# A mixture-of-experts tail: picks sorted by expert, two rows a token fetched during the last experts, the other four fetched 32 tokens at a time and summed in four PSUM strips

## The reference

```
scores = sigmoid(h2d @ w_router)                    # (1056, 64), float32
eidx   = top 6 of (scores + bias) inside the best 4 of 8 groups
w      = scores[eidx] / sum(scores[eidx]) * 2.5
routed[t] = sum_k w[t, k] * swiglu(h2d[t], w_gate[e], w_up[e], w_down[e]),  e = eidx[t, k]
out = layer_norm(2 ** 0.25 * h + routed + swiglu(h2d, shared weights))
```

## Time and profile before

| what | value |
|---|---|
| median of 3 plain runs | 1801.19 us (1797.17 to 1805.35) |
| the profiled execution | 1811.97 us |
| its span, first to last instruction | 1809.8 us |
| PE busy | 1740.8 us, 96% of the span |
| DVE busy | 1069.2 us, 59% |
| ACT busy | 678.6 us, 37% |
| POOL busy | 331.7 us, 18% |
| moved by the DMA engines | 409.01 MB, mean 226 GB/s |
| mean granted clock of PE | 0.988 of full |

### The profile page before, as it was taken

The page is one execution under the profiler, slowest core; times in us unless marked ns, Lnnn a source line. Parts: engine busy times, 40 slices in busy tenths (PEclk is TensorE's granted clock), DMA queues, the critical chain, the costliest instruction groups (busy, mean ns, idle before and its releaser), DMA issues. The chain is left out here.

```text
span 1809.8 us, 27145 instructions
## 1 busy us (share of the span) xinstructions
PE 1740.8 (96%) x9472; PEld 1336.0 (74%) x9472; DVE 1069.2 (59%) x1724; ACT 678.6 (37%) x1092; POOL 331.7 (18%) x282
## 2 busy tenths in 40 slices
PE   9999999999999999999996889999999999999996
PEld 9999999999955555998873556767676767676633
DVE  3112442634345565745684657777777777777568
ACT  3112222312244555212110145656565656565411
POOL 0000321412010000000145332222222222222112
PEclk9999999999999999999997999999999999999998
DMA  6332633434223123624260589999999999999697
GB/s 223 93 93 76 169 118 108 145 118 136 74 67 102 40 67 136 244 83 156 92 239 1 181 293 374 394 379 404 396 407 382 398 393 384 397 396 366 226 376 315
DMA packets 140736, 409.01 MB, mean 226 GB/s; under 512 B 29444, under 2 KB 91300, under 8 KB 121060
## 3 DMA queue, kind: packets, MB, share of 16 engines
q1 hardware_dynamic: 116436, 338.38, 50.8%
q0 software_dynamic: 21344, 52.59, 7.6%
q10 hardware_dynamic: 2880, 17.04, 2.3%
HBM read 359.78 MB, written 67.80 MB: 236 GB/s over the span
## 5 line engine op out<-in xcount | busy, mean ns | idle before, releaser
L2675 PE MATMUL e_Y<-mixT,e_aT 128*128 128x512 f32 x544 | 246.7, 596 | 6.8 <-issue 5.8
L2686 PE MATMUL e_G<-w_lo,xT_hi 128*128 128x512 f32 x528 | 205.7, 390 | 0.0
L2675 PEld LDWEIGHTS e_Y<-mixT,e_aT 128*128 128x128 f32 x544 | 103.5, 191 | 112.1 <-issue 107.0
L2533 DVE TENSOR_TENSOR w_lo<-wb,e_w_hi 128x1024 fp32r<-128x1024 f32 x132 | 155.5, 1220 | 16.4 <-ACT e_w_hi L2453 9.5
L2526 DVE TENSOR_TENSOR xT_lo<-e_T,xT_hi 128x1024 fp32r<-128x1024 f32 x66 | 80.8, 1225 | 133.3 <-ACT xT_hi L2448 133.3
L2533 DVE TENSOR_TENSOR w_lo<-wb,half_hi 128x1024 fp32r<-128x1024 f32 x128 | 150.7, 1220 | 10.4 <-ACT half_hi L2453 10.2
L1323 PE MATMUL banks<-x_hi,gw_hi 128*128 128x352 f32 x464 | 151.6, 327 | 1.4 <-DVE r_srg L1115 1.4
L1323 PE MATMUL banks<-x_hi,gw_lo 128*128 128x352 f32 x464 | 148.8, 321 | 0.0
L1323 PE MATMUL banks<-x_lo,gw_hi 128*128 128x352 f32 x464 | 148.8, 321 | 0.0
L2448 ACT CAST xT_hi<-e_T 128x1024 fp32r<-128x1024 f32 x66 | 67.1, 1017 | 206.8 <-PE e_T L2664 206.8
L187 PE MATMUL banks<-w_hi,x_hi 128*128 128x244 f32 x512 | 142.0, 277 | 1.6 <-DVE x_lo L244 1.6
(11 more groups left out here) (436 smaller groups left out, 3604.2 us busy)
## 6 DMA issues: line engine op xcount, KB each, us to landing
wb<-in_w_exp_gu SPq DMA_DIRECT2D x64, 2048.0 KB
mixT<-in_w_exp_dn SPq DMA_DIRECT2D x68, 1024.0 KB
yk<-d_y_rows SPq DMA_DIRECT2D x16, 1536.0 KB, 18.9
gw_sb<-in_w_gate SPq DMA_DIRECT2D x20, 512.0 KB, 7.0
d_proj<-o_sb SPq DMA_DIRECT2D x8, 1098.0 KB, 5.6
d_gateT<-r_g_out ACTq DMA_DIRECT2D x16, 528.0 KB, 2.6
pages<-in_cache_both SPq DMA_DIRECT2D x64, 128.0 KB, 2.0
wb<-in_w_exp_gu ACTq DMA_DIRECT2D x4, 2048.0 KB
```

The lines of the kernel that those rows point to most:

```text
L2533: v.tensor_tensor(w_lo[s][:, :, at_k, :], w_gu[s][:, :, at_k, :], w_hi[c][:, :, at_k, :].bitcast(F32), ALU.subtract).then_inc(w_lo_ok, 1)
L2675: mm = t_.matmul(Y[q][:], aT[:, c, k, :], w_d[:, s, k, q * 512:(q + 1) * 512], start=k == 0, stop=k == 1)
L2686: mm = t_.matmul(G[c], x[:, c, k, :], w[:, :, k, :], start=k == 0 and i == 0, stop=k == KD - 1 and i == 2)
```

## The change

1. `choose` sorts the six picks of a token by expert number, largest first (a copy to float and a MAX8 for each tile). So picks 4 and 5 never belong to the last four experts.
2. The overflow blocks run before the last four experts (60 to 63) and no longer after them. The lists are rearranged on DVE for that.
3. Picks 4 and 5 of each tile (`pair`, one transfer of 1 MB) are loaded during the last group, once the rows of the first 64 blocks have landed, and DVE adds them (`add_row`) at several places: one add after the second block's gated(), three before the last gated(), four around the last two evacuations, eight behind them.
4. Picks 0 to 3 of each tile (`stack`, four transfers of 512 KB) are loaded when all rows have landed. A transfer takes 32 tokens x 4 picks onto 128 partitions, so that partition 4 * token + pick holds one row. PE multiplies such a block with a 128x32 matrix w_stack, in which column i holds the four weights of token i, into 32 PSUM partitions (a strip); four blocks make the tile. Seven stack buffers lie over those of the pairs and the weights; some wait until pairs are added.
5. w_stack is made by DVE (w_masked, before the last group), four small products on PE with a constant matrix `sel` (loaded once, 0.28 MB), and DVE (`stacked_weights`, before the last evacuations). The diagonal matrices (`diag`, L2637) are gone.
6. LAST_ORDER is now 0 to 8, the small tile last; its six transfers come behind all stacks. h tiles 0 and 1 are loaded in trunk in the place of the norm's constants, and the constants during the last group, in the place of those.

```diff
-LAST_ORDER = (NT - 1, *range(NT - 1))
+LAST_ORDER = range(NT)
...
-            sp.dma_start(g1, a["ln2_g"].partition_broadcast(P)).then_inc(ln2_in, 16)
-            sp.dma_start(b1, a["ln2_b"].partition_broadcast(P)).then_inc(ln2_in, 16)
+            for t in range(2):
+                sp.dma_start(early[:, t * D:(t + 1) * D], h_rows[tok(t), :]).then_inc(acc_in[t], 16)
...
-                link(v.tensor_copy(f6[:].rearrange("p (t k) -> p t k", k=TOPK), i8[:, :, 0:TOPK]))
+                link(v.tensor_copy(f8[:, :, 0:TOPK], i8[:, :, 0:TOPK]))
+
+                for t in range(G):
+                    ins = v.max(by_number[:, t, :], f8[:, t, :])
+                link(ins)
+                link(v.tensor_copy(f6[:].rearrange("p (t k) -> p t k", k=TOPK), by_number[:, :, 0:TOPK]))
...
+            def pair(t):
+
+                sp.dma_start(pairs[t][:].rearrange("p k n -> p (k n)"),
+                             y_rows.rearrange("(t k) n -> t (k n)", k=8)[t * P:(t + 1) * P, 4 * D:6 * D]).then_inc(pair_in[t], 16)
+
+            def stack(t):
+
+                b = stack_of[t][0]
+                for q in range(4):
+                    sp.dma_start(stacks[b][:, q, :], y_rows.rearrange("(t k) n -> t k n", k=8)[t * P + NS * q:t * P + NS * (q + 1), 0:4, :]).then_inc(stack_in[b], 16)
...
+            weights_read(0)
+            rows_written(NE - W)
+            pair(0)
+            pair(1)
+            wait_alone(sp, x_turned, sp.snap(more * (2 * W) + 2 * (NE - W + 2)))
+            pair(2)
+            weights_read(1)
+            pair(4)
+            pair(5)
+            down_read(0)
+            h_tile(2)
+            h_tile(3)
+            wait_alone(sp, x_turned, sp.snap(more * (2 * W) + 2 * NE))
+            pair(3)
+            weights_read(2)
+            pair(6)
+            pair(7)
+            down_read(1)
+            h_tile(4)
+            h_tile(5)
+            down_read(2)
+            h_tile(6)
+            h_tile(7)
+            h_tile(NT - 1)
+            down_read(3)
+            sp.dma_start(g2, a["ln2_g"].partition_broadcast(P)).then_inc(ln2_in, 16)
+            sp.dma_start(b2, a["ln2_b"].partition_broadcast(P)).then_inc(ln2_in, 16)
+            weights_read(3)
+            rows_written(NE)
+            for t in range(3):
+                stack(t)
+            for t in range(3, NT - 2):
+                pair_added(2 * t - 5)
+                stack(t)
+            sp.wait_ge(pe_done, 1)
+            stack(NT - 2)
+            for k in range(TOPK):
+                small(k)
...
+                    if last and s == W - 2:
+                        small_weights()
+                    if last and s == W - 1:
+                        for t, k in ((0, 5), (1, 4), (1, 5)):
+                            add_row(t, k)
                     gated(at(dve, r, W, s + 1), c)
+                    if last and s == 1:
+                        add_row(0, 4)
...
+            stacked_weights()
             wait_alone(dve, y_out[0], at(dve, r, 8 * W, -16))
             take_out(at(dve, r, W, -2), 2)
             kept(at(dve, r, W, -1), 0)
+            for t, k in ((2, 4), (2, 5), (3, 4)):
+                add_row(t, k)
             wait_alone(dve, y_out[1], at(dve, r, 8 * W, -16))
             take_out(at(dve, r, W, -1), 3)
             kept(at(dve, r, W, 0), 1)
...
+            add_row(3, 5)
...
+            for t in range(4, NT - 1):
+                add(t)
...
+            pe.wait_ge(sel_in, 16)
+            pe.wait_ge(masked_ok, 1)
+            for k in range(4):
+                mm = t_.matmul(AS[:, 1, 0:4 * (NT - 1)], sel[:, P * k:P * (k + 1)], w_masked[:, k].rearrange("p q t -> p (q t)"), start=k == 0, stop=k == 3)
+            mm.then_inc(quarter_ok, 1)
             four(pe.snap(more + (NE // W - 1)), last=True)
...
-                for k in range(ON_PE):
-                    for c in range(2):
-                        mm = t_.matmul(S[i % 4][:, c, :], diag[:, t, k, :], yk[i % 4][:, k, c * 512:(c + 1) * 512], start=False, stop=k == ON_PE - 1)
+                b, use = stack_of[t]
+                pe.wait_ge(stacked_ok, 1)
+                pe.wait_ge(stack_in[b], 64 * use)
+                for c in range(2):
+                    for q in range(4):
+                        mm = t_.matmul(S[i % 4][NS * q:NS * (q + 1), c, :], w_stack[:, q, t, :], stacks[b][:, q, c * 512:(c + 1) * 512], start=False, stop=True)
                 mm.then_inc(pe_done, 1)
```

More of the change, by code:

```diff
@@ L2242, in _, with experts @@
             mm.then_inc(e_gu_done, 1)
-def experts(nc, passed, begun, parts, acc_in, acc, yk_in, yk_rest, yk, junk, shared, ident, wb, gu_in, ready, w_d, d_in, early, ln2_in, a, h_rows, tok_list, meta, y_rows, out_p, out_s):
+def experts(nc, passed, begun, parts, acc_in, acc, pair_in, pairs, stack_in, stacks, w_stack, sel, small_rows, junk, shared, ident, wb, gu_in, ready, w_d, d_in, ln2, ln2_in, a, h_rows, tok_list, meta, y_rows, out_p, out_s):
     with ExitStack() as ctx:
@@ L2338, in _ @@
             sp.wait_ge(over_clear, 1)
-            with sp.Fori(2, OVER // W + 2) as r:
+            with sp.Fori(2, OVER // W) as r:
                 for s in range(W):
@@ new lines, in add_row @@
+            def add_row(t, k):
+                assert (t, k) == (n_added[0] // 2, 4 + n_added[0] % 2)
+                if t not in tile_added:
+                    dve.wait_ge(acc_in[t], 16)
+                else:
+                    dve.wait_ge(added, tile_added[t])
+                dve.wait_ge(pair_in[t], 16)
+                v.scalar_tensor_tensor(acc[t][:], pairs[t][:, k % 2, :], w_part[:, t, k:k + 1], acc[t][:], ALU.mult, ALU.add).then_inc(added, 1)
+                n_added[0] += 1
+                tile_added[t] = n_added[0]
@@ new lines, in add, with stacked_weights, small_weights @@
+            def add(t):
+                add_row(t, 4)
+                add_row(t, 5)
+            def stacked_weights():
+                dve.wait_ge(quarter_ok, 1)
+                v.tensor_tensor(w_stack[:].rearrange("p q t n -> p (q t) n"), sel[:, 4 * P:4 * P + NS].unsqueeze(1).broadcast_to([P, 4 * (NT - 1), NS]),
+                                AS[:, 1, 0:4 * (NT - 1)].unsqueeze(2).broadcast_to([P, 4 * (NT - 1), NS]), ALU.mult).then_inc(stacked_ok, 1)
+            def small_weights():
+                dve.wait_ge(part_ok, 1)
+                for k in range(TOPK):
+                    own = slice(NS * (k % 4), NS * (k % 4 + 1))
+                    dve.wait_ge(small_w_ok, k + 1)
+                    v.tensor_scalar(diag_small[own, k // 4, :], ident[own, own], w_small[own, k // 4:k // 4 + 1], None, ALU.mult).then_inc(small_ok, 1)
@@ L2758, in _ @@
             shared_down(2)
-            for i in range(NT):
-                if i == 0:
+            routed(0)
+            routed(1)
+            for i in range(2, NT):
+                if i < NT - 1:
+                    routed(i)
+                else:
                     routed_small()
-                else:
-                    routed(i)
-                if 1 <= i and i + 3 < NT:
-                    shared_down(i + 3)
+                if i + 2 < NT:
+                    shared_down(i + 2)
 def program(nc, a, o):
```

187 lines of the change are left out of this document (93 added, 94 removed).

## The result

The changed kernel takes 1784.52 us (median of 6 plain runs, 1783.96 to 1790.36), the kernel before 1802.45 us in the same session (1797.17 to 1805.35). The ratio is 0.9911, 95% interval 0.9893 to 0.9930: 17.9 us or 0.9% faster. Forecast were 1783.5 us (1774 to 1797) and "faster" at 0.85.

The account below looks back on a forecast made before the run. Three nearly level engines (PE, DMA, DVE) were taken to bound the end; -23.6 behind the last scatter's landing, +3.9 for its later landing, +1.0 and +1.0 make -17.7 us, from 1801.2 to 1783.5 us, range 1774 to 1797.

Parts of the forecast that it names:

- The three levels: At the end of the kernel PE, DMA engines and DVE are nearly level, so a gain needs all three to fall.
- Strips: Weighted sum on PE: products in four strips cost about 1.85 us a tile instead of 5.15, plus 0.2 for alternation.
- Rival (a): Strips run one after another: 10.3 us a tile, end at T0 (last scatter's landing) + 93, 1814 us; chance 0.05.
- Sort: Sorting the picks in choose(): only the third batch shows, +1.0 us, range 0 to 5.
- Quarter matmuls: Ahead of the last four experts PE does four small products of 128x128 by 32 columns: +1.0 us.
- The wait of add_row(0, 4): In the last four experts DVE's first add waits for its late pair, and PE loses 1.9 us.
- Last scatter: The last scatter carries a full expert's rows under loaded queues: +1.5 us, bounds 0.4 and 4.
- Loads moved ahead: Pair loads, seven and a quarter h tiles, norm constants and four scatters, about 15 MB, fill the queues from 1693 to about 1728.
- The loads: Behind the last scatter's landing (T0): 2 us latency, 4.9 us a tile, eighth stack at T0 + 41, small rows T0 + 44.4.
- Rival (b): Loads become the bound at 283 GB/s: 1799 us, no change; decides below some 390 GB/s; chance 0.09.
- Clock: While PE waits for stacks in the tail its granted clock falls once: +2.4 us.
- Tail: Behind PE's end: join, mean, root and scaled for tiles 7 and 8, then the last output, 10.5 us.

Follow-up runs that it names:

- Pairs late: Changed kernel with the eight pair loads sent only after the last scatter and all sixteen adds behind the last evacuation: 1791.26 us, ratio 0.9996 to the kernel before.
- One strip: Changed kernel with all eight products of a tile given to the first PSUM strip, then six repeated in the other three: 1819.18 us, ratio 1.0097 to the kernel before.
- two queues: Changed kernel with ACT's queue sending half of the first three stacks' loads beside SP's: 1785.31 us, ratio 0.9904; a second such kernel also finishes the small tile earlier: 1788.83 us.
- the three kernels with the old end: The kernel before, that kernel with only the sort (ratio 1.0002), and with the sort and the overflow blocks moved ahead of the last four experts (1.0038).
- changed, again: The changed kernel run once more, unchanged, on the same chip as three other kernels: 1783.11 us, ratio 0.9888 to the kernel before.
- the constants late: Changed kernel with the two loads of the norm's constants sent behind the first three stacks: 1787.00 us, ratio 0.9900 to the kernel before.
- The sort with the new order: Kernel before with the sort in choose() and the overflow blocks moved ahead of the last four experts, tail as before: 1798.21 us, ratio 1.0038 to the kernel before.
- half of the loads: Changed kernel with two of each stack's four loads left out and the first two used twice: 1776.60 us, ratio 0.9842 to the kernel before.
- the sort alone: Kernel before with only the sort in choose() added: 1791.82 us against 1791.61, ratio 1.0002.
- the exchanged loops: Changed kernel with the two loops of routed() exchanged, so neighbouring products use the same strip: 1776.72 us, ratio 0.9918 to the kernel before.

## Why the prediction was right, step by step

**The three levels.** "A gain needs all three to fall" held, and the runs say more. Pairs late has the strips and the shorter DVE list, and gains nothing. One strip has the earlier pairs and is 15 us slower than the kernel before (1819.18 against 1804.13). The 8.4 MB of pair loads moved ahead are worth the whole gain (14.5 us in plain runs, 16.9 to 18.1 us of tail, 1.5 of it the clock), and the strips keep PE from eating it up.

**Strips.** Forecast 1.85 us a tile and 0.2 for the change of shape; measured 1.92 and a step of 5.48 us, the very figure. The change of shape shows in the shared product, 3.63 us from its start to that of the next (1745.45 to 1749.08), where two shared products in a row are 3.43 apart. The Trainium skill (TensorEngine Tiling, Key Properties) states that changing the mode drains the engine. In this trace the wide product pays 0.2 us; what a narrow group may pay within its 1.85 us no run separates. Rival (a) was priced at 10.3 us a step and T0 + 93; forced, it is 10.66 us and T0 + 99 (107.0 less a scatter of 7.9), above the forecast because the first product began at T0 + 9.0 and not 7, the first tile ran at the low clock (9.8 us from its start to the next instead of 6.9), and the step was too small by 0.36.

**Sort.** Forecast +1.0 us; 0.5 by the trace, 0.2 with an interval of about 2 us either way by its own run. The range up to 5 us, taken from late instructions, was not needed: they aren't there in the profile after.

**Quarter matmuls.** Forecast 1.0 us. The chain of the changed kernel has eight records at 1664.60 with 0.81 us. Right.

**The wait of add_row(0, 4).** Forecast: pair 0 late by some 4 us, PE loses 1.9. In the profiled execution DVE waits 2.20 us and PE nothing. The step that failed is the row from which the scatter ahead was priced: after the new order block 64 is an overflow block with hardly any rows (0.47 MB before, 0.00 MB now), whose scatter was sent at 1679.54 and had landed by 1681.88, in 2.3 us instead of 4.5. Few rows aren't all of it: in the two kernels with two queues the same empty scatter took 3.96 and 3.73 us, against 2.2 to 2.7 in the kernels with one queue, and why is open. The mechanism itself is real. In the kernel with two queues the wait was longer, and there the forecast chain shows (waits of DVE and of PE in the last blocks: us, times, longest):

```profile
DVE early L2644 <- DMA pair<-d_y_rows: 3.9, 1, 3.9
PE e_G L2783 <- DVE w_lo L2594: 0.8, 1, 0.8
PE e_Y L2772 <- DVE pages L2599: 0.7, 1, 0.7
```

3.9 us on DVE make 1.5 us on PE; 2.2 to 2.8 us in the kernels with one queue and early pairs make 0 to 0.6. From the eighth-last scatter's start to the last one's, the three kernels with the old end (one of them in the new order) take 60.88 or 60.89 us. The changed kernel takes 62.00 and, again, 62.24, pairs late 61.78, and the kernel with two queues 63.72. So the quarter, this wait and the later adds together cost 1.1 us in the changed kernel's profile and up to 2.8 with two queues, where 1.0 + 1.9 + 0.5 = 3.4 were forecast.

**Last scatter.** Forecast +1.5, measured +3.6 (7.71 against 4.11), the largest error of size. Two parts show on one chip: a full expert's rows make 5.23 of 3.42 us (+1.8, about the +1.5 forecast for all of it), and the pairs in the queues another 1.8 (7.64 with them, 5.86 without). The constants have little part in it (7.45). The forecast left out the second part. The bytes moved between the last scatter's start and its landing say more about it: the scatters' queue moved 0.72 MB there in the changed kernel (0.70 with the constants late), and 0.46 MB, its own rows, with pairs late and in the sort with the new order. So with early pairs 0.26 MB of the scatter before it were still to be written, and the last one came behind them. That this order is what delays it is argued from the bytes; no run separates it.

**Loads moved ahead.** The prediction's list has seven and a quarter h tiles; the change sends six and a quarter there (h tiles 0 and 1 are loaded in trunk). It changes nothing: from 1686 to 1710 us the DMA share was 1.00 to 1.03, as the sign for it said.

**The loads.** Forecast: 4.9 us a tile, eighth stack at T0 + 41, "PE, no longer the DMA, is last there by 2 to 3 us". This step failed: the eighth stack was waited for until 1766.00, T0 + 47.8. In the first 8 us only 252 and 331 GB/s moved, against 410 later (0.9 MB, 2.3 us, where 2 were taken as latency). The first stack was there at T0 + 9.0 and not at 6.9, since parts of the next ones move beside it: 2.7 MB had moved by then, and a stack is 2.1. A tile needs 2.10 MB / 0.410 = 5.1 us. The small rows and the first output, forecast to come behind, share the last stretch (1.2 MB besides the stacks until 1766, at 309 GB/s between 1760 and 1764 us). It is the loads that bind: 8.6 us less work of PE moves the tail by -0.3 us, half of the loads by -7.5, and then PE binds. Rival (b) was right in its mechanism and wrong in its size, since the rate was 410 GB/s and not 283; its threshold of 390 was met with little to spare. The Trainium skill (DMA: Bandwidth & Descriptors, Specifications) gives about 358 GB/s for one core, worked out as half of a memory stack's 716 GB/s for two cores. This kernel runs on one core, and its trace does not agree: 407 to 416 GB/s over 30 us.

**Clock.** Forecast one loss of 2.4 us. The loss is there (3.64 + 3.52 where twice 1.92 would do, 3.3 us), but it falls into time in which PE would wait for the next stack anyway and costs nothing. The two errors offset each other, by luck: PE's continuous work was forecast from T0 + 16.9 plus 2.4 for the clock, and its third product began at that very T0 + 19.3, but because the third stack landed late. The forecast of the end was T0 + 62.8, the result T0 + 63.7. The sort with the new order shows what the same loss costs where no load hides it, 1.65 us.

**Tail.** Forecast 10.5 us behind PE's end, measured 10.0 (1771.90 to 1781.9).

**Sum.** Tail, -19.1 us (90.5 to 71.4; -20.0 from the sort alone to the exchanged loops, on one chip); sort, quarter, wait and order, +1.6 to +3.3. That makes -15.8 to -18.4 us. Forecast were -22.1 for the tail (90.5 to 62.8 + 5.6) and +4.4 for the rest. So the tail gained 3.0 us less than forecast and the rest lost 2.8 us less (in the profiled execution, +1.6): that the sum came out within 0.2 us is luck. The plain runs say -17.9, and on two of the other chips -15 (exchanged loops) and -20 (changed, again). What differs lies in the stretches ahead of the tail, which vary by several microseconds between executions.

## What to carry to other kernels

When several engines are level, a kernel changes its bound and not only its time: ask after each edit which loads remain behind the last dependency, and leave out half of one engine's work to see whether anything moves. Narrow products belong in different PSUM strips, where four cost little more than one; in one strip each costs a full product. A tile that is small in partitions is not small for VectorE, so the last product should be a long one under which the chain of the tile before can finish.

## What the hardware showed that was not expected

Eight products with 128x32 weights and 512 columns, two to each of four strips, take 1.92 us, and 1.94 with the same strip twice in a row. Six more in other strips, issued behind eight in one, hide completely under them (6.87 us): products of other strips begin before the last ones of strip 0, which were issued ahead of them.

The last scatter took 3.4 or 4.1 us from issue to landing with hardly any rows, and 5.2, 5.9 or 7.7 us with a full block's (0.46 MB). Taking 1 MB of loads out of the queue just ahead of it hardly shortened it (7.45), though the engines' share then was 0.52 and 0.15 in its last 3.4 us.
